# Joint attention: the samples' score products as sixteen tiles of 32 by 32 at once, over four PSUM banks

## The chip, the core and the metric

The kernel runs on one core of one Trainium2 chip. The metric is the device time of one execution, in microseconds. The kernel before took 3689.43 us in the median of three runs (3681.23 to 3694.0).

## The reference

One inference step of a two-layer streaming encoder. Layer 0 holds sliding-window attention beside differential attention (4 heads of two score maps each), layer 1 holds forgetting attention (16 heads), and each layer has a SwiGLU block. A prompt of 1024 new frames and 8 running sample streams go through the same weights. Each sample stream brings 16 new frames and a cache of 2048 keys and values. What the change touches is the sample side of the two global attentions:

```python
def _diff_attend(q, k, v, qpos, kpos, lam):          # layer 0, part B
    scores = jnp.einsum('bthed,bshed->bhets', q2, k2).astype(jnp.float32) * SCALE
    p = jax.nn.softmax(jnp.where(mask, scores, NEG_INF), axis=-1)
    attn = p[:, :, 0] - lam * p[:, :, 1]
    return jnp.einsum('bhts,bshd->bthd', attn.astype(v.dtype), v)

def _fox_attend(q, k, v, cq, ck, qpos, kpos):        # layer 1
    scores = jnp.einsum('bthd,bshd->bhts', q, k).astype(jnp.float32) * SCALE
    scores = scores + jnp.moveaxis(cq, 1, 2)[..., :, None] - jnp.moveaxis(ck, 1, 2)[..., None, :]
    p = jax.nn.softmax(jnp.where(mask, scores, NEG_INF), axis=-1)
    return jnp.einsum('bhts,bshd->bthd', p.astype(v.dtype), v)
```

The products meant by the title are `q k^T` of one stream's 16 frames, for eight half-heads or heads (128 rows), with its 2048 cached keys. In layer 1 a fifth product adds the forget bias.

## The kernel before

`joint_attention` is called twice: as `jb` (differential, `diff` true) and as `jc` (forgetting attention). It interleaves the prompt's attention of one head with the cached attention of one sample stream. Such a pair is called a unit `u` here: `U` is 8 in `jb` and 16 in `jc`. Each unit has S = 8 steps `s`, one for each 128-row tile of the prompt's head, in the order 3, 4, 2, 5, 1, 6, 0, 7. With n = 8u + s, a step issues on TensorE (PE): `score(n + 3)`, `turn(n + 1)` (transposes of the probabilities, groups of four into a slot of the ring `turned`, which has 2 PSUM banks), on odd steps `attend((n - 1) // 2)` (probabilities times values, for two tiles at once), on even steps `turn_back((n - 2) // 2)`.

The sample's work is put between these. In unit u the products with the cached keys (`score_keys`) run at s = 6 and 7, and the rest for that stream follows in unit u + 1: ScalarE (ACT) copies the scores to SBUF (`copy_scores`: the first pair at s = 7, the second at s = 0), VectorE (DVE) takes the maximum at s = 1, ACT the exponential at s = 2 and 3, PE transposes and multiplies by the values from s = 3 to s = 5 (`turn_probs`, `attend_sample`), DVE scales the output at s = 6 (`scale_output`), PE turns it at s = 7 (`turn_output`) and DVE copies it out at s = 7 (`copy_out`).

`score_keys(u, pair)` issues, for each of 4 (`jb`) or 5 (`jc`) inner steps, matmuls of 32 rows by 32 columns for the four column groups c and the two row groups a of the pair: eight tiles, into the two banks of `s_ps`. Each matmul of the code is two in the trace. The same two banks hold the sample's transposed probabilities and its output later, so the second pair waits for the copies of the first.

DVE also transposes the cached keys of the next stream by 32 by 32 blocks (`turn_keys`, 16 instructions for a unit): four at each of s = 5, 6 and 7, two at each of s = 3 and 4; unit 0 has six at s = 6 and at s = 7, and in the last unit there are none. Half of a step's transposes stand before `invert`, half after it, all in front of the next step's work:

```python
                    if n % 2 == 1:
                        output((n - 3) // 2)
                    if 1 <= u <= U and s == 6:
                        scale_output(u - 1)
                    maximum(n + 3)
                    turns = turns_at(u, s)
```

Each engine works in the order of its code. `attend(k)` waits for `out_done` 2k (L1517), that is for DVE's `output(k - 1)`, which stands at the head of DVE's same odd step and itself needs PE's `turn_back(k - 1)` of the step before. SyncE issues the loads of keys when `s_done` says that `score_keys` of two units back has ended, and the loads of values when `s_pv_done` says that `attend_sample` has.

## Time and profile before

| | us |
|---|---|
| runs: median (lowest to highest of 3) | 3689.43 (3681.23 to 3694.0) |
| span of the profiled execution | 3685.0 |
| PE busy (all) | 3411.1 (93%) |
| DVE busy | 1597.5 (43%) |
| ACT busy | 1123.5 (30%) |
| matmuls of L1556 (`score_keys`), busy, `jb` and `jc` | 59.6 and 123.3, with the bias's 38.0 |
| `jc`, from the first to the last block of `score_keys` | 537.95 |

The page is read from the top: PE is busy nearly the whole span, so the questions are which of PE's work becomes shorter, and what PE would wait for then. A group's busy time is the union of its instructions' spans, which overlap where tiles run side by side; so the length of a block is read from the starts in the timeline, not from the mean of one.

### The profile page before, as it was taken

The numbers are of one execution on the slowest core, as the hardware profiler recorded it, in microseconds if no ns is written. First come the engines' busy times: TensorE is split into PE (matmuls) and PEld (weight loads), VectorE is DVE, ScalarE is ACT, GpSimd is POOL, SyncE is SP. The second block draws the span as 40 slices with busy tenths as digits, with TensorE's granted clock in tenths as the row PEclk, the third lists the DMA queues.
The fourth block names the chain that finished last, engine by engine and source line by source line (L and its number), as shares of the span: only waits on it lengthen the run. The fifth ranks groups of instructions, "written<-read, shape, count | busy, mean of one in ns | idle before, by whom it ended". The sixth has DMA issues, their size and how long they took to land. (4 is left out here: it accounts for less than half of the span.)

```text
span 3685.0 us, 63062 instructions
## 1 busy us (share of the span) xinstructions
PE 3411.1 (93%) x25000; PEld 2914.6 (79%) x25000; DVE 1597.5 (43%) x2910; ACT 1123.5 (30%) x2343; POOL 254.4 (7%) x340
## 2 busy tenths in 40 slices
PE   8998599788999999997899799999988999999997
PEld 7876466577999999996789666666567999999996
DVE  5417477463333333336231266666533333333334
ACT  4215255443112112113222245555433211211211
POOL 2310000032000000004000000000013000000003
PEclk9999799999999999998999899999989999999999
DMA  5438599443111111112554599999644111111102
GB/s 170 127 122 181 168 336 309 159 161 119 36 34 57 34 46 34 39 41 92 154 174 124 148 317 320 303 308 329 213 149 137 43 37 34 57 34 46 34 29 102
DMA packets 399665, 493.23 MB, mean 134 GB/s; under 512 B 69744, under 2 KB 251536, under 8 KB 399312
## 3 DMA queue, kind: packets, MB, share of 16 engines
q1 hardware_dynamic: 399456, 490.36, 42.8%
q8 instruction: 141, 2.31, 0.3%
q14 instruction: 68, 0.56, 0.1%
HBM read 407.10 MB, written 84.10 MB: 133 GB/s over the span
## 5 line engine op out<-in xcount | busy, mean ns | idle before, releaser
L2546 DVE TENSOR_TENSOR f_gated<-f_gated,f_up 128x384 f32<-128x384 f32 x132 | 73.1, 554 | 734.8 <-ACT f_gated L2476 734.8
L2570 DVE TENSOR_TENSOR f_y<-f_y,f_down 128x512 f32<-128x512 f32 x396 | 269.5, 686 | 229.6 <-PE f_down L2665 229.5
L2652 PE MATMUL f_gate<-m_ht_hi,f_w_hi 128*128 128x384 f32 x1056 | 355.0, 336 | 12.1 <-DVE f_w_lo L2597 12.1
L2652 PE MATMUL f_gate<-m_ht_lo,f_w_hi 128*128 128x384 f32 x1056 | 354.5, 336 | 0.0
L2652 PE MATMUL f_gate<-m_ht_hi,f_w_lo 128*128 128x384 f32 x1056 | 354.5, 336 | 0.0
L2652 PE MATMUL f_up<-m_ht_hi,f_w_lo 128*128 128x384 f32 x1056 | 352.7, 334 | 0.0
L2652 PE MATMUL f_up<-m_ht_hi,f_w_hi 128*128 128x384 f32 x1056 | 352.7, 334 | 0.0
L2652 PE MATMUL f_up<-m_ht_lo,f_w_hi 128*128 128x384 f32 x1056 | 352.7, 334 | 0.0
L2665 PE MATMUL f_down<-f_wo_hi,f_act_hi 128*128 128x512 f32 x792 | 312.6, 395 | 10.7 <-DVE f_y L2570 9.3
L2665 PE MATMUL f_down<-f_wo_lo,f_act_hi 128*128 128x512 f32 x792 | 309.2, 390 | 0.0
L2665 PE MATMUL f_down<-f_wo_hi,f_act_lo 128*128 128x512 f32 x792 | 309.1, 390 | 0.0
L2476 ACT ACTIVATE f_gated<-f_gate 128x384 f32<-128x384 f32 x132 | 65.0, 493 | 684.6 <-PE f_up L2652 684.3
L2652 PEld LDWEIGHTS f_gate<-m_ht_hi,f_w_hi 128*128 128x128 f32 x1056 | 199.6, 189 | 13.7 <-issue 12.9
L2652 PEld LDWEIGHTS f_gate<-m_ht_lo,f_w_hi 128*128 128x128 f32 x1056 | 199.6, 189 | 0.8
L2652 PEld LDWEIGHTS f_gate<-m_ht_hi,f_w_lo 128*128 128x128 f32 x1056 | 199.5, 189 | 0.0
L2652 PEld LDWEIGHTS f_up<-m_ht_hi,f_w_lo 128*128 128x128 f32 x1056 | 198.2, 188 | 0.0
L2652 PEld LDWEIGHTS f_up<-m_ht_hi,f_w_hi 128*128 128x128 f32 x1056 | 198.2, 188 | 0.0
L2652 PEld LDWEIGHTS f_up<-m_ht_lo,f_w_hi 128*128 128x128 f32 x1056 | 198.2, 188 | 0.0
L2665 PEld LDWEIGHTS f_down<-f_wo_hi,f_act_hi 128*128 128x128 f32 x792 | 149.2, 188 | 52.6 <-DVE f_y L2570 19.0
L1822 DVE STREAM_TRANSPOSE jc_kc<-jc_kc 128x512 f32<-128x512 f32 x256 | 180.9, 706 | 16.8 <-DMA jc_kc<-in_cache_c_k 2.7
L2665 PEld LDWEIGHTS f_down<-f_wo_hi,f_act_lo 128*128 128x128 f32 x792 | 148.9, 188 | 31.6
L2665 PEld LDWEIGHTS f_down<-f_wo_lo,f_act_hi 128*128 128x128 f32 x792 | 149.0, 188 | 29.6
(394 smaller groups left out, 6698.8 us busy)
## 6 DMA issues: line engine op xcount, KB each, us to landing
jc_kc<-in_cache_c_k SPq DMA_DIRECT2D x64, 1024.0 KB, 10.5
jc_vc<-in_cache_c_v SPq DMA_DIRECT2D x64, 1024.0 KB, 10.3
jb_kc<-in_cache_b_k SPq DMA_DIRECT2D x32, 1024.0 KB, 11.6
jb_vc<-in_cache_b_v SPq DMA_DIRECT2D x32, 1024.0 KB, 11.1
m_raw<-in_w_ffn_in SPq DMA_DIRECT2D x44, 512.0 KB
f_raw<-in_w_ffn_in SPq DMA_DIRECT2D x44, 512.0 KB
f_raw_o<-in_w_ffn_out SPq DMA_DIRECT2D x22, 1024.0 KB, 6.4
m_raw<-x SPq DMA_DIRECT2D x18, 512.0 KB, 4.1
```

The source lines that it names most:

```text
L1822: dve.transpose(kc[:, u % 2, t, :], kc[:, u % 2, t + 1, :]).then_inc(kt_done, 1)
L2476: act.activation(silu[:, b], gate[:, q, 0:gw], ACT.Silu).then_inc(silu_done, 1)
L2546: dve.tensor_tensor(prod[:, b], silu[:, b], up[:, q, 0:gw], ALU.mult).then_inc(prod_done, 1)
L2570: dve.tensor_tensor(part, part, down[:, half, :], ALU.add).then_inc(added, 1)
L2652: last = pe.matmul(acc[:, q, 0:gw], a[:, s, k, u, :], b[:, k, token], start=(k == 0 and j == 0), stop=(k == KT - 1 and j == 2))
L2665: last = pe.matmul(down[:, half, :], a[:, s, t * P:(t + 1) * P], b[:, s, half * 512:(half + 1) * 512], start=(n == 0), stop=(n == 5))
```

## The change

`score_keys(u)` is called once, at s = 7, with all four row groups: sixteen tiles for each inner step, into four banks. Two of these are the banks of `s_ps`, two are slots of the ring `turned`, used under new keys `("sk", u, 0)` and `("sk", u, 1)`. ACT copies all four banks at s = 0 of the next unit, the ring's two first, ahead of that step's `copy_prompt`. `turn_output` goes from s = 7 to s = 6 and writes to `s_ps` instead of a ring slot, with semaphores of its own (`ot_done`, `ot_copied`). DVE's `copy_out` stays at s = 7 but goes ahead of that step's transposes, and `score_keys(u)` waits for it.

```diff
--- before.py
+++ after.py
@@ -1226,8 +1226,9 @@
             use_prompt(S * u + s + 1)
             if u < U and s == 5:
                 use(("sn", u), "act")
-            if 1 <= u <= U and s == 7:
-                use(("ot", u - 1), "dve", 1 if diff else 2)
+            if u < U and s == 7:
+                use(("sk", u, 0), "act")
+                use(("sk", u, 1), "act")
     use(("fin", 0), "dve")
     use(("fin", 1), "act")
     key_at = {r: key for key, r in seq.items()}
@@ -1267,9 +1268,10 @@
...
+         scaled, ot_done, ot_copied, s_stored) = (st.sem(n) for n in (
...
+        out_ops = 1 if diff else 2
@@ -1537,15 +1539,16 @@
                         last = pe.matmul(o_back[:, e * DH:(e + 1) * DH], src[0:held], halves[0:held], start=True, stop=True)
                 last.then_inc(back_done, 1)
 
-            def score_keys(u, pair):
-                if pair == 0:
-                    pe.wait_ge(kt_done, parts * per * (u + 1))
-                    if u:
-                        pe.wait_ge(scaled, u)
-                pe.wait_ge(s_copied, 4 * u + 2 * pair)
-                for step in range(4 if diff else 5):
+            def score_keys(u):
+                pe.wait_ge(kt_done, parts * per * (u + 1))
+                if u:
+                    pe.wait_ge(scaled, u)
+                    pe.wait_ge(ot_copied, out_ops * u)
+                banks = [ring_slot(("sk", u, 0)), ring_slot(("sk", u, 1)), s_ps[:, 0], s_ps[:, 1]]
+                n_steps = 4 if diff else 5
+                for step in range(n_steps):
                     for c in range(4):
-                        for a in (2 * pair, 2 * pair + 1):
+                        for a in range(4):
                             rows_a, hb = slice(Q * a, Q * a + Q), 4 * c + step
                             if step < 4:
                                 weights = q_blocks[rows_a, hb // 2, hb % 2]
@@ -1553,10 +1556,11 @@
                             else:
                                 weights = select[rows_a, Q * c:Q * c + Q]
                                 moving = bias[rows_a, u % 2, 0:bank].rearrange("p (t r) -> p t r", r=Q)
-                            last = pe.matmul(s_ps[Q * c:Q * c + Q, a % 2].rearrange("p (t r) -> p t r", r=Q), weights, moving,
-                                             start=(step == 0), stop=(step == (3 if diff else 4)), skip_group_check=True,
+                            last = pe.matmul(banks[a][Q * c:Q * c + Q].rearrange("p (t r) -> p t r", r=Q), weights, moving,
+                                             start=(step == 0), stop=(step == n_steps - 1), skip_group_check=True,
                                              tile_position=(Q * a, Q * c))
-                last.then_inc(s_done, 1)
+                            if step == n_steps - 1 and c == 3:
+                                last.then_inc(turn_done if a < 2 else s_done, 1)
 
             def score_new(u):
                 if u == 0:
@@ -1584,7 +1588,7 @@
             def turn_probs(u, gi):
                 a, b = PG[gi]
                 pe.wait_ge(s_exp_done, 2 * u + (1 if b <= per * 2 else 2))
-                pe.wait_ge(s_copied, 4 * (u + 1))
+                pe.wait_ge(s_copied, 2 * (u + 1))
                 if gi >= 2:
                     pe.wait_ge(pt_copied, len(PG) * u + (1, 3, 4)[gi - 2])
                 for t in range(a, b):
@@ -1596,7 +1600,7 @@
             def attend_sample(u, part):
                 pe.wait_ge(pt_copied, len(PG) * u + (2, 4)[part])
                 if part == 0:
-                    pe.wait_ge(s_copied, 4 * (u + 1))
+                    pe.wait_ge(s_copied, 2 * (u + 1))
                 else:
                     pe.wait_ge(vnew_loaded, 16 * (u + 1))
                 for t in ((range(0, 2 * per), range(2 * per, tiles))[part]):
@@ -1615,7 +1619,8 @@
 
             def turn_output(u):
                 pe.wait_ge(scaled, u + 1)
-                pe.transpose(ring_slot(("ot", u))[:, 0:P], o_rows[:], ident[:]).then_inc(turn_done, 1)
+                pe.wait_ge(pt_copied, len(PG) * (u + 1))
+                pe.transpose(s_ps[:, 0, 0:P], o_rows[:], ident[:]).then_inc(ot_done, 1)
 
             pe.wait_ge(setup, 10)
             score(0)
@@ -1637,18 +1642,18 @@
                     if 1 <= u <= U and s == 5:
                         turn_probs(u - 1, 4)
                         attend_sample(u - 1, 1)
-                    if u < U and s >= 6:
-                        score_keys(u, s - 6)
+                    if u < U and s == 7:
+                        score_keys(u)
                     if n % 2 == 0:
                         turn_back((n - 2) // 2)
                     if 1 <= u <= U and s == 4:
                         attend_sample(u - 1, 0)
                         turn_probs(u - 1, 2)
-                    if 1 <= u <= U and s == 7:
+                    if 1 <= u <= U and s == 6:
                         turn_output(u - 1)
             for part in range(2):
                 slot = ring_slot(("fin", part))
-                wait_emptied([("ot", U - 1)])
+                pe.wait_ge(ot_copied, out_ops * U)
                 for j in range(pairs // 2):
                     last = pe.transpose(slot[:, j * P:(j + 1) * P], out_t[:, part * pairs // 2 + j, :], ident[:])
                 last.then_inc(turn_done, 1)
@@ -1702,13 +1707,17 @@
                     act.wait_ge(back_done, k)
                 act.activation(o_turn[:], pv[:, 0:2 * P], ACT.Copy).then_inc(o_copied, 1)
 
-            def copy_scores(u, pair):
-                act.wait_ge(s_done, 2 * u + pair + 1)
+            def copy_scores(u, a):
+                if a < 2:
+                    act.wait_ge(turn_done, seq[("sk", u, a)] + 1)
+                else:
+                    act.wait_ge(s_done, 2 * (u + 1))
                 if u:
                     act.wait_ge(pt_done, len(PG) * u)
-                for a in (2 * pair, 2 * pair + 1):
-                    act.activation(s_scores[:, 0:PAST].rearrange("p (t a r) -> p a t r", a=4, r=Q)[:, a],
-                                   s_ps[:, a % 2].rearrange("p (t r) -> p t r", r=Q), ACT.Copy).then_inc(s_copied, 1)
+                dst = s_scores[:, 0:PAST].rearrange("p (t a r) -> p a t r", a=4, r=Q)[:, a]
+                src = turned[:, seq[("sk", u, a)] % ring] if a < 2 else s_ps[:, a - 2]
+                act.activation(dst, src.rearrange("p (t r) -> p t r", r=Q), ACT.Copy).then_inc(
+                    act_emptied if a < 2 else s_copied, 1)
 
             def copy_new_scores(u):
                 if u:
@@ -1733,18 +1742,20 @@
             for u in range(U + 1):
                 for s in range(S):
                     n = S * u + s
-                    if u < U and s == 7:
-                        copy_scores(u, 0)
                     exponential(n + 2)
                     if n % 2 == 0:
                         copy_output((n - 2) // 2)
                     if u >= 1 and s == 3:
                         exponential_sample(u - 1, 1)
+                    if u >= 1 and s == 0:
+                        copy_scores(u - 1, 0)
+                        copy_scores(u - 1, 1)
                     copy_prompt(act, n + 1)
                     if diff and u == 0 and s == 7:
                         exponential_lambda()
                     if u >= 1 and s == 0:
-                        copy_scores(u - 1, 1)
+                        copy_scores(u - 1, 2)
+                        copy_scores(u - 1, 3)
                     if u >= 1 and s == 2:
                         exponential_sample(u - 1, 0)
                     if u >= 1:
@@ -1828,11 +1839,13 @@
                 dve.transpose(ktn, kn).then_inc(ktn_done, 1)
 
             def maximum_sample(u, x):
-                dve.wait_ge(s_copied, 4 * u + 2 * x + 2)
+                if x == 0:
+                    dve.wait_ge(act_emptied, count[("sk", u, 1)])
+                else:
+                    dve.wait_ge(s_copied, 2 * (u + 1))
                 if u and x == 0:
                     dve.wait_ge(s_exp_done, 2 * u)
                 if x == 0:
-                    dve.wait_ge(act_emptied, count[("sn", u)])
                     dve.tensor_reduce(s_neg[:, 2:3], s_scores[:, PAST:], AX.X, ALU.max, negate=True).then_inc(s_max_done, 1)
                 part = s_scores[:, 0:PAST].rearrange("p (t x n) -> p x t n", x=2, n=2 * Q)[:, x]
                 dve.tensor_reduce(s_neg[:, x:x + 1], part, AX.XY, ALU.max, negate=True).then_inc(s_max_done, 1)
@@ -1850,7 +1863,7 @@
                 dve.wait_ge(s_pv_done, u + 1)
                 dve.wait_ge(s_inv_done, u + 1)
                 if u:
-                    dve.wait_ge(turn_done, seq[("ot", u - 1)] + 1)
+                    dve.wait_ge(ot_done, u)
                 if diff:
                     dve.tensor_scalar(o_rows[:], o_ps, s_inv[:, u % 2:u % 2 + 1], weight[:], ALU.mult,
                                       ALU.mult).then_inc(scaled, 1)
@@ -1858,19 +1871,19 @@
                     dve.tensor_scalar(o_rows[:], o_ps, s_inv[:, u % 2:u % 2 + 1], None, ALU.mult).then_inc(scaled, 1)
 
             def copy_out(u):
-                key, g = ("ot", u), u // STREAMS
-                o_turn = turned[:, seq[key] % ring, 0:P].rearrange("p (j e f) -> p j e f", j=4, e=2)
-                dve.wait_ge(turn_done, seq[key] + 1)
+                g = u // STREAMS
+                o_turn = s_ps[:, 0, 0:P].rearrange("p (j e f) -> p j e f", j=4, e=2)
+                dve.wait_ge(ot_done, u + 1)
                 if diff:
                     dve.tensor_copy(o_first_head[:], o_turn[:, :, 0, :]).then_inc(o_half, 1)
                     dve.wait_ge(o_half, u + 1)
                     dve.tensor_tensor(out_t[:, 4 * g:4 * g + 4, frames_of(u)], o_first_head[:], o_turn[:, :, 1, :],
-                                      ALU.add).then_inc(dve_emptied, 1)
+                                      ALU.add).then_inc(ot_copied, 1)
                 else:
                     for hd in range(2):
                         part = slice(DH * hd, DH * hd + DH)
                         dve.tensor_scalar(out_t[part, 4 * g:4 * g + 4, frames_of(u)], o_turn[part, :, hd, :], 1.0, None,
-                                          ALU.mult).then_inc(dve_emptied, 1)
+                                          ALU.mult).then_inc(ot_copied, 1)
 
             def products_lambda():
                 dve.wait_ge(lam_loaded, 32)
@@ -1898,6 +1911,8 @@
                     if 1 <= u <= U and s == 6:
                         scale_output(u - 1)
                     maximum(n + 3)
+                    if 1 <= u <= U and s == 7:
+                        copy_out(u - 1)
                     turns = turns_at(u, s)
                     for v, t in turns[:len(turns) // 2]:
                         turn_keys(v, t)
@@ -1919,8 +1934,6 @@
                     invert(n)
                     for v, t in turns[len(turns) // 2:]:
                         turn_keys(v, t)
-                    if 1 <= u <= U and s == 7:
-                        copy_out(u - 1)
             copy_turned(dve, ("fin", 0), s_out[:, 0:pairs * P // 2], turned[:, seq[("fin", 0)] % ring, 0:pairs * P // 2])
 
 
```

## Rows read from the trace of the kernel before

**Rows 1.** the page: granted TensorE clock in 40 slices, in tenths

```profile
PEclk9999799999999999998999899999989999999999
```

**Rows 2.** windows: length, busy of PE, PEld, DVE, ACT, POOL; clock, DMA share, GB/s

```profile
2128.25:2666.20 537.95, 518.43 (x7536) 340.12 (x7543) 346.98 (x781) 281.95 (x693) 0.00 (x0) 0.99 0.94 299
```

**Rows 3.** timeline of PE, jc, steps 6, 7: start, duration, ..., [idle before]

```profile
2311.66 3.66 PE L1556 MATMUL jc_s_ps<-jc_kc,jc_q_blocks 32*32 32x512 f32 x64
2315.12 1.06 PE L1556 MATMUL jc_s_ps<-jc_bias,jc_select 32*32 32x512 f32 x16
2316.11 0.66 PE L1537 MATMUL jc_pv<-jc_halves,jc_o_turn 128*128 128x64 f32 x4
...
2317.63 1.30 PE L1522 MATMUL jc_pv<-jc_probs_t,jc_vp 128*64 128x256 f32 x16
2318.86 3.66 PE L1556 MATMUL jc_s_ps<-jc_kc,jc_q_blocks 32*32 32x512 f32 x64
...
2323.31 0.33 PE L1618 MATMUL jc_turned<-jc_ident,jc_o_rows 128*128 128x128 f32 x1
```

**Rows 4.** timeline of PEld (weight loads), jc, start of a block

```profile
2128.25 0.18 PEld L1556 LDWEIGHTS jc_s_ps<-jc_kc,jc_q_blocks 32*32 32x32 f32 x16 [0.17 <-issue]
```

**Rows 5.** timeline of DVE, jc, the same steps 6 and 7

```profile
2310.88 0.82 DVE L1768 TENSOR_REDUCE jc_neg_top<-jc_scores_b 128x1 f32<-128x640 f32 x1 [0.54 <-PE jc_scores_b L1496]
...
2313.25 1.53 DVE L1822 STREAM_TRANSPOSE jc_kc<-jc_kc 128x512 f32<-128x512 f32 x2
2316.81 0.48 DVE L1803 TENSOR_SCALAR jc_out<-jc_pv,jc_inv 128x64 f32<-128x64 f32 x2 [2.03 <-PE jc_pv L1537]
...
2323.68 0.48 DVE L1872 TENSOR_SCALAR jc_out_t<-jc_turned 64x64 f32<-64x64 f32 x2 [2.76 <-PE jc_turned L1618]
```

**Rows 6.** timeline of PE, jb: a block at step 6 and what follows

```profile
562.79 3.66 PE L1556 MATMUL jb_s_ps<-jb_kc,jb_q_blocks 32*32 32x512 f32 x64
566.38 0.44 PE L1534 MATMUL jb_pv<-jb_ident,jb_o_turn 128*128 128x128 f32 x2
...
567.61 2.23 PE L1522 MATMUL jb_pv<-jb_probs_t,jb_vp 128*128 128x256 f32 x16
```

**Rows 7.** timeline of PE, jb, step 7 of unit 0

```profile
462.20 2.23 PE L1522 MATMUL jb_pv<-jb_probs_t,jb_vp 128*128 128x256 f32 x16 [0.62 <-DVE jb_out L1803]
```

**Rows 8.** timeline of DVE, jb, beside rows 6

```profile
564.49 1.52 DVE L1822 STREAM_TRANSPOSE jb_kc<-jb_kc 128x512 f32<-128x512 f32 x2
566.86 0.61 DVE L1799 SCALAR_TENSOR_TENSOR jb_out<-jb_pv,jb_inv_lam,jb_out 128x128 f32<-128x128 f32 x2 [0.85 <-PE jb_pv L1534]
```

**Rows 9.** timeline of ACT, jc: the copies of both pairs of scores

```profile
2316.29 1.09 ACT L1710 ACTIVATE jc_s_scores<-jc_s_ps 128x512 f32<-128x512 f32 x2 [3.81 <-PE jc_s_ps L1556]
...
2325.61 1.09 ACT L1710 ACTIVATE jc_s_scores<-jc_s_ps 128x512 f32<-128x512 f32 x2
```

**Rows 10.** timeline of PE, jc, step 3: first transposes of probabilities

```profile
2331.38 1.09 PE L1593 MATMUL jc_s_ps<-jc_ident,jc_s_scores 128*128 128x128 f32 x8 [0.90 <-ACT jc_s_scores L1723]
```

**Rows 11.** windows: five single units, columns as in rows 2

```profile
2139.90:2174.04 34.14, 33.24 (x499) 22.13 (x491) 22.73 (x50) 18.68 (x46) 0.00 (x0) 1.00 1.05 320
2289.11:2323.31 34.20, 33.30 (x500) 22.28 (x493) 23.20 (x52) 18.68 (x46) 0.00 (x0) 1.00 0.93 302
2323.31:2357.65 34.34, 33.44 (x501) 22.30 (x494) 23.20 (x52) 18.68 (x46) 0.00 (x0) 1.00 1.01 323
573.40:607.60 34.20, 32.94 (x449) 23.98 (x444) 23.70 (x52) 18.74 (x46) 0.00 (x0) 1.00 1.04 341
607.60:642.10 34.50, 33.07 (x451) 24.03 (x444) 25.16 (x60) 18.79 (x46) 0.00 (x0) 1.00 0.93 300
```

**Rows 12.** timeline of PE, jc: two idle stretches before a matmul

```profile
2226.63 0.21 PE L1578 MATMUL jc_turned<-jc_turned_new,jc_q_blocks 32*32 32x16 f32 x3 [2.13 <-issue]
...
2236.05 6.21 PE L1556 MATMUL jc_s_ps<-jc_kc,jc_q_blocks 32*32 32x512 f32 x54 [1.86 <-issue]
```

**Rows 13.** window after the second of these, columns as in rows 2

```profile
2236.00:2249.00 13.00, 12.95 (x98) 5.38 (x100) 2.78 (x8) 3.02 (x7) 0.00 (x0) 0.50 1.00 257
```

3 lines of the change are left out of this document (1 added, 2 removed).

## The prediction

> **What bounds the kernel now.** The windows over the `jc` stage come first [rows 2]: PE is busy 518 of 538 us, the DMA engines have a share of 0.94, DVE 347 us, ACT 282 us. So PE sets the time, and DMA is the next. The timeline of PE over steps 6 and 7 of one unit is the second view [rows 3]. The reader is to see two blocks of `score_keys`, each 4.45 us from its own start to that of the next work (2311.66 to 2316.11, 2318.86 to 2323.31). Five inner steps of two matmuls each give ten rounds of eight tiles, and the rows of 64 and 16 matmuls are ten times eight. In `jb` there are eight rounds and a block takes 3.59 us (562.79 to 566.38) [rows 6]. The difference of two rounds is 0.86 us, so a round costs 0.43 us, and 0.15 us or so of a block is its start. The granted clock is 1.00, its upper level of 2.4 GHz, in every single unit read [rows 11]; the slices of the whole span show it a little lower only here and there [rows 1].
>
> **What the change removes.** The sixteen tiles of an inner step run in one round where they were two of eight. If the array takes the four row groups at once as it now takes two, one of the two blocks of a unit is gone whole: 4.45 us in each of 16 units of `jc`, 3.59 us in each of 8 of `jb`, 71.2 + 28.7 = 99.9 us of PE time. No row shows four row groups at work. What speaks for it: four banks are written by four row groups, one each, as two are by two now, and sixteen weight loads of this shape go in 0.18 us [rows 4], less than half of a round. I take one round for sixteen, 0.43 us; the other end is 0.86 us, as before.
>
> The Trainium skill ("TensorEngine Tiling (Array Packing)", sections "Tiling Modes" and "Restrictions and Gotchas") says that the 32 by 32 mode has sixteen tiles which load and multiply in parallel, and that different row tiles must write to different PSUM banks, which the change obeys. By it the block is halved as above; no run here shows it yet. The same page ("PSUM Bottleneck") warns that the copies out of PSUM may then become the bound.
>
> **Where it is put, and what was hidden there.** The block that goes is, in time, the one at step 6, because all tiles now run at step 7. It covered DVE. At step 7 `attend` waits for DVE's `output`, which stands behind four key transposes of step 6. Before, the pair of transposes at 2313.25 ended at 2314.78, the block ended at 2316.11, and DVE was idle for 2.03 us until `turn_back` gave it work [rows 5]. Now PE passes from the end of step 6's `turn` (2311.66) to `attend` in the time that `turn_back`, `score` and `turn` took, 2317.63 - 2316.11 = 1.52 us, and 0.09 us for `turn_output`: it is there at 2313.27. DVE is free at 2314.78, `output` takes 0.48 us [rows 5], and about 0.1 us passes until PE starts: 2315.36. PE waits 2.1 us, so a unit of `jc` gains 4.45 - 2.1 = 2.35 us.
>
> In `jb` PE reaches `attend` at 562.79 + (567.61 - 566.38) + 0.09 = 564.11 [rows 6]. The transposes end at 566.01 and `output` takes 0.61 us [rows 8], so PE starts at about 566.7: 2.6 us of wait, and a gain of 3.59 - 2.6 = 1.0 us. That this wait is real shows in unit 0 of `jb`, where six transposes stand at step 6: PE already waits 0.62 us for `output` there, with the block still in place [rows 7].
>
> **The units at the ends.** Unit 0 has six transposes at that place, so in `jb` nothing is gained and in `jc` I take 0.5 us. The last unit has none, so the whole block is gained: 4.45 and 3.6 us. The sum: `jc` 14 x 2.35 + 4.45 + 0.5 = 37.9 us, `jb` 6 x 1.0 + 3.6 + 0 = 9.6 us, together 47.5 us.
>
> **What is moved, and its cover.** `copy_out` (0.48 us [rows 5]) now stands ahead of step 7's transposes, and the block waits for it. DVE does `output` until 2315.3, a maximum over 384 columns (0.82 us for 640, so about 0.5) and `copy_out` until 2316.3; PE's `attend` runs from 2315.36 for 1.23 us to 2316.6. So this costs nothing, with a margin of 0.3 us in `jc`; in `jb` `attend` is 0.9 us longer [rows 6] and the margin over 1 us. Were the margin gone, it would cost at most the 0.5 us a unit, 11 us in all. Step 7's transposes are later by 0.48 us and still end before step 0's maximum is due. `turn_output` at step 6 waits for `scaled`, which DVE gives before its maximum at 2310.88; nothing.
>
> ACT copied the first pair under the second block (idle before it 3.81 us), and the second 2.30 us after that block's end, behind `copy_prompt` [rows 3, 9]. Now all four copies follow the block. A pair takes 1.09 us. The ring's two start 0.18 us after the end, as at 2316.29 after 2316.11, and are done at 1.27 us. PE meanwhile has step 0's `score` to do, needs the first slot only then, and the second four transposes later, so it waits less than that 1.27 us, and I take nothing. `copy_prompt` then copies two groups; at the 0.55 us of one of these copies it is done by 2.37 us, and the other pair at 3.46 us behind the block, where it ended 3.39 us behind it before (2326.70 - 2323.31). So the chain over DVE's maximum to ACT's exponential, which lets PE wait 0.90 us at step 3 [rows 10], keeps its length. Bounds: nothing, or the 1.09 us of the pair in each of 24 units, 26 us. I take nothing, because the later end comes out the same.
>
> The skill's warning on the copies would make those 26 us the result; the rows on ACT speak against it, since ACT is busy 18.7 of 34.2 us of a unit [rows 11].
>
> **DMA, the next bound.** A window under steady load shows a share of 1.05 [rows 11], so I take that as full. Two `jc` units in a row have 0.93 and 1.01, thus 31.7 us of full load for each on the mean; two of `jb` 1.04 and 0.93, thus 32.2 us. The forecast makes a unit 34.2 - 2.35 = 31.9 us in `jc` and 33.3 us in `jb`. It just fits. The loads have buffers for a unit ahead, so I take nothing here, but DMA is the reason why a larger gain would not come through: if the wait for `output` were not there, units would stop at 31.7 and 32.2 us, a gain of 2.6 and 2.1 us each.
>
> **Clock.** PE now idles for 2.1 to 2.6 us in 20 units. In this trace the clock held at 1.00 over 2.13 us of idle; the next idle, listed with 1.86 us, was followed by 0.50, its lower level of 1.2 GHz, for 13 us [rows 12, 13]. Half of that, 6.5 us, is lost by one such fall. So the new idle stretches lie just where the trace shows both results. Bounds: no fall, or one in each of the 20 units, 130 us. I take one in five, 4 falls, as the first row held and the second had that idle 10 us ahead of it; and 4 us for each, since the new block has half as many rounds to slow. That is 16 us, an estimate.
>
> **The sum.** 47.5 - 16 = 31.5 us. From the profiled 3685.0 us that gives a span of 3653.5 us; the median of the runs lies 4.4 us above that span, so the forecast is 3689.4 - 31.5 = 3658 us.
>
> **The rivals.**
> A. Less of the wait, DMA at the limit. If PE waits less for DVE than I think, DMA stops the gain: 15 x 2.6 + 4.45 + 7 x 2.1 + 3.6 = 61.8 us, and no fall of the clock: 3628 us. For it speaks that the wait is worked out and seen only in unit 0; against it the fixed order of DVE's work.
> B. The clock falls often. Place: the wait at step 7. Price 6.5 us for each fall; from 7 falls on nothing is left of the gain, and with 14 the time is 3689.4 - 47.5 + 91 = 3733 us, slower than before. For it speaks [rows 12, 13]; against it that 2.13 us held.
> C. Sixteen tiles take two rounds, so the change doesn't do what it says. The block then takes the time of two, nothing is removed but the start of one (0.15 us a unit), and the wait for `output` remains new: 14 x 2.1 + 6 x 2.6 - 24 x 0.15 = 41 us more, 3731 us. It turns slower from a round of about 0.63 us on (47.5 us over 24 units is 2.0 us, over 8 to 10 rounds 0.2 us).
> D. The pieces cancel: 4 to 7 falls at full price, or the copies on the chain (26 us), leave 3680 to 3695 us.
>
> **How the numbers follow.** Forecast 0.60, A 0.15, B 0.08, C 0.07, D 0.10. The range goes from A's time to where D ends, 3628 to 3695 us, which leaves out B and C. The bound for faster and slower is 0.3%, about what a measurement of this kernel can tell from no change: 3678 and 3700 us. Faster: forecast and A, 0.75. Slower: B and most of C, 0.14. Same: 0.11.
>
> **What would show it right or wrong.** One block of `score_keys` a unit, with 128 and 32 matmuls merged, 4.45 us long in `jc` and 3.6 in `jb` (C: 8.7 us). At step 7 `attend` with an idle of about 2.1 us (2.6 in `jb`) before it, released by DVE's `output`, in all units but the last (A: under 1 us). The wait at step 3 still 0.9 us. A `jc` unit of 31.9 us with a DMA share near 1.05 (A: waits for DMA appear on DVE's transposes). The granted clock under 1.00 in some windows of single units (B: in most). The prediction is wrong at its root if `attend` at step 7 does not wait, or if the block is not halved.

## The result: 3697 us, a little slower than before

The changed kernel takes 3697.0 us (median of 18 runs, 3691.5 to 3707.5) where the kernel before takes 3688.8 us (18 runs, 3679.8 to 3698.7): a ratio of 1.0026, 95% interval 1.0017 to 1.0036. The forecast was 3658 us with a range to 3695, so it missed, on the side of slower. The profiled execution has a span of 3696.7 us (3685.0 before), and the page's slices of the granted clock stand against [rows 1]:

```profile
core 0: 3696.7 us, clock 0.955
PEclk9999699989999999998899889999989999999999
```

Two windows answer to [rows 2]: from the end of the first block of `score_keys` to the end of the last one, in `jb` (7 units) and in `jc` (15 units). Columns as in rows 2. The kernel before (from the end of its first pair of blocks):

```profile
467.95:709.81 241.86, 230.28 (x3087) 166.42 (x3079) 161.97 (x382) 128.99 (x315) 0.00 (x0) 1.00 0.88 290
2139.90:2667.27 527.37, 507.85 (x7373) 335.32 (x7365) 337.45 (x763) 277.95 (x683) 0.00 (x0) 0.99 0.94 299
```

The changed kernel:

```profile
472.76:717.13 244.37, 215.01 (x3084) 169.05 (x3080) 161.01 (x384) 129.69 (x315) 0.00 (x0) 0.99 0.85 281
2151.77:2679.56 527.79, 471.56 (x7370) 338.24 (x7365) 334.65 (x765) 282.16 (x683) 0.00 (x0) 0.96 0.92 295
```

The halving is there: PE is busy 36.3 us less in `jc` and 15.3 us less in `jb`. But the stretches are as long as before (+0.4 and +2.5 us), because PE's idle time went from 19.5 to 56.2 us and from 11.6 to 29.4 us. The waits of PE in the `jc` window say for whom (total us, times, longest). Before:

```profile
PE jc_s_ps L1593 <- ACT jc_s_scores L1723: 13.5, 15, 0.9
PE jc_s_ps L1556 <- issue: 2.2, 2, 1.9
PE jc_turned L1578 <- issue: 2.1, 1, 2.1
PE jc_s_ps L1611 <- issue: 0.9, 2, 0.6
PE jc_pv L1522 <- DVE jc_out L1803: 0.7, 1, 0.7
```

After, the four largest:

```profile
PE jc_pv L1524 <- DVE jc_out L1814: 28.6, 15, 2.2
PE jc_s_ps L1597 <- ACT jc_s_scores L1732: 13.5, 15, 0.9
PE jc_turned L1559 <- issue: 5.2, 4, 2.4
PE jc_s_ps L1559 <- issue: 4.0, 3, 2.3
```

The wait for ACT is the same 13.5 us. The wait of `attend` for DVE's `output` is new, 27.9 us more. "issue", the wait for nothing that the profile shows, goes from 5.2 to 13.9 us over all its rows. One unit of `jc` shows both (timeline of PE, steps 6 and 7, as in [rows 3]):

```profile
2358.87 0.61 PE L1507 MATMUL jc_turned<-jc_ident,jc_probs 128*128 128x128 f32 x4
2361.64 1.11 PE L1524 MATMUL jc_pv<-jc_probs_t,jc_vp 128*64 128x256 f32 x14 [2.17 <-DVE jc_out L1814]
...
2369.01 0.62 PE L1559 MATMUL jc_turned<-jc_kc,jc_q_blocks 32*32 32x512 f32 x2 [1.77 <-issue]
...
2371.09 0.50 PE L1496 MATMUL jc_scores_b<-jc_k_both,jc_q_hi 128*128 128x512 f32 x1
```

DVE beside it, as in [rows 5]:

```profile
2357.99 1.52 DVE L1833 STREAM_TRANSPOSE jc_kc<-jc_kc 128x512 f32<-128x512 f32 x2
2359.43 0.12 DVE L1788 RECIPROCAL jc_inv<-jc_total 128x1 f32<-128x1 f32 x1
2359.61 1.53 DVE L1833 STREAM_TRANSPOSE jc_kc<-jc_kc 128x512 f32<-128x512 f32 x2
2361.07 0.43 DVE L1814 TENSOR_SCALAR jc_out<-jc_pv,jc_inv 128x64 f32<-128x64 f32 x2
```

`output` stands behind four key transposes, and `attend` starts 0.57 us after `output` does: the predicted wait, 2.17 us where 2.1 was forecast. The block then has a stop of 1.77 us in its middle, for nothing that the profile names; and this block of sixteen tiles takes 8.24 us in all, where a block of eight took 4.45. The stop costs more than its idle time: an undisturbed block is 5.45 us (below), 1.77 more make 7.22, and this one is another 1.02 us longer at a granted clock of 1.00. Over the stops in blocks at full clock, in this kernel and in e1_turns, that surplus is 0.5 to 1.0 us each.

**A round of sixteen.** An undisturbed block, the last of `jc`, shows what is left when nothing stops it (timeline of PE; the first tile of each of the first four rounds, and the work behind the block):

```profile
2674.12 0.62 PE L1559 MATMUL jc_turned<-jc_kc,jc_q_blocks 32*32 32x512 f32 x2
...
2674.57 0.59 PE L1559 MATMUL jc_turned<-jc_kc,jc_q_blocks 32*32 32x512 f32 x2
...
2675.00 0.80 PE L1559 MATMUL jc_turned<-jc_kc,jc_q_blocks 32*32 32x512 f32 x2
...
2675.43 0.80 PE L1559 MATMUL jc_turned<-jc_kc,jc_q_blocks 32*32 32x512 f32 x2
...
2679.57 0.69 PE L1539 MATMUL jc_pv<-jc_halves,jc_o_turn 64*128 64x64 f32 x3
```

It takes 2679.57 - 2674.12 = 5.45 us, 1.00 us more than the 4.45 of a block of eight; in `jb` it is 4.39 for 3.59 us. All sixteen do run at once. But ten rounds need 5.45 and eight need 4.39, so a round is 0.53 us on the mean, not 0.43. The first tiles of the rounds shown still follow each other by 0.43 to 0.45 us; from the third round on it is the tiles behind them that come late. The weight loads show where (timeline of PEld, same block):

```profile
2674.57 0.10 PEld L1559 LDWEIGHTS jc_turned<-jc_kc,jc_q_blocks 32*32 32x32 f32 x1 [0.23 <-issue]
2675.00 0.29 PEld L1559 LDWEIGHTS jc_turned<-jc_kc,jc_q_blocks 32*32 32x32 f32 x2 [0.33 <-issue]
2675.21 0.10 PEld L1559 LDWEIGHTS jc_s_ps<-jc_kc,jc_q_blocks 32*32 32x32 f32 x1
```

Before, in a block of eight tiles:

```profile
2311.66 0.18 PEld L1556 LDWEIGHTS jc_s_ps<-jc_kc,jc_q_blocks 32*32 32x32 f32 x16 [0.17 <-issue]
2312.11 0.12 PEld L1556 LDWEIGHTS jc_s_ps<-jc_kc,jc_q_blocks 32*32 32x32 f32 x3 [0.28 <-issue]
2312.41 0.28 PEld L1556 LDWEIGHTS jc_s_ps<-jc_kc,jc_q_blocks 32*32 32x32 f32 x13 [0.18 <-issue]
```

With eight tiles a whole group of sixteen loads (0.18 to 0.28 us) is done under the matmuls ahead of it. With sixteen, one single load goes ahead (2674.57) and one more at 2675.00; the others begin only some 0.2 us later, when the matmuls before have ended, and then loads and matmuls come one pair after another.

The Trainium skill ("TensorE: Matmul & The Clock Gate", section "Part 3: Packing small matmuls — row/col tiling") says that PE pulls weight loads ahead of running matmuls out of a window of 64 instructions. Two rounds of sixteen are 32 loads and 32 matmuls, 64 instructions, and two rounds of eight are 32; the rows agree with that, without showing the window itself. A rival, that the array or the banks are slower with more than eight tiles and the loads only follow, is not excluded by these rows.

### The profile page after: what moved, and what is told of

Read it like the earlier page. It is cut to its first block and busy times, and to the rows that moved or that the text cites. A ratio compares the mean times of both kernels' runs of the same rounds, so it can differ in the third digit from the quotient of the medians.

```text
span 3696.7 us, 63126 instructions
## 1 busy us (share of the span) xinstructions
PE 3363.5 (91%) x25000; PEld 2928.5 (79%) x25000; DVE 1591.8 (43%) x2910; ACT 1128.8 (31%) x2343; POOL 254.8 (7%) x340
## 3 DMA queue, kind: packets, MB, share of 16 engines
q8 instruction: 141, 2.31, 0.3%
## 5 line engine op out<-in xcount | busy, mean ns | idle before, releaser
L2665 PEld LDWEIGHTS f_gate<-m_ht_hi,f_w_hi 128*128 128x128 f32 x1056 | 199.6, 189 | 13.7 <-issue 12.9
L2678 PEld LDWEIGHTS f_down<-f_wo_hi,f_act_lo 128*128 128x128 f32 x792 | 149.2, 188 | 31.5
```

Source lines behind the costliest of these rows:

```text
L2665: last = pe.matmul(acc[:, q, 0:gw], a[:, s, k, u, :], b[:, k, token], start=(k == 0 and j == 0), stop=(k == KT - 1 and j == 2))
L2678: last = pe.matmul(down[:, half, :], a[:, s, t * P:(t + 1) * P], b[:, s, half * 512:(half + 1) * 512], start=(n == 0), stop=(n == 5))
```

## The experiments

Times are medians, ratios are against the kernel before on the same chip. "Stage" is the `jc` window from the end of the first block to that of the last, 15 units: 527.4 us before, 527.8 us after. Three theories on where the 39 us between forecast and result went are tested: W, sixteen tiles at once leave no room for weight loads ahead, so a round is 0.53 us; C, the wait for `output` also makes the clock fall; F, the stops inside the blocks are waits for instructions, whose fetches the bulk loads delay.

**e1_turns: the four transposes moved away.** The table of key transposes alone is changed, so that none stands ahead of `output` at step 6:

```
-    ahead = {5: range(0, 4), 6: range(4, 8), 7: range(8, 12), 3: range(12, 14), 4: range(14, 16)}
+    ahead = {5: range(0, 4), 7: range(4, 12), 3: range(12, 14), 4: range(14, 16)}
```

> The four key transposes that DVE did at step 6 are done at step 7, behind copy_out and under the block of score products. Theory D (DVE's output stands behind these transposes, PE waits for it ahead of attend, and the wait makes the clock fall): the wait of 2.18 us in jc and 2.5 to 2.6 us in jb goes to under 0.5 us in all units but the first, where six transposes stay at step 6. The falls of the clock inside the two stages (2 in jb, 12 in jc, 3.4 us each) go to 3 or fewer. About 38 us of waits and 14 x 1.7 = 24 us of clock come back: 3697 - 60 = 3637 us, between 3625 and 3655. Rival (DMA is the bound of both kernels in these stages, so the units stay at 34 to 35 us whatever PE waits for): the same wait appears elsewhere, on DVE for keys or on PE for values, and the time stays within 3690 to 3700 us.

Measured 3662.2 us (3658.6 to 3670.8, 4 runs), ratio 0.993 (0.9911 to 0.9949): faster than both kernels. The wait of `attend` is gone in every unit but the first and last of a stage. So the wait was caused by the order of DVE's work. But 25 us of the expected gain are missing: the stage takes 509.2 us.

```profile
2132.91:2642.12 509.21, 463.65 (x7371) 335.33 (x7366) 339.56 (x765) 280.95 (x683) 0.00 (x0) 0.98 0.96 305
```

The stops inside the blocks have grown. The longest (timeline of PE):

```profile
2161.26 0.60 PE L1559 MATMUL jc_turned<-jc_kc,jc_q_blocks 32*32 32x512 f32 x2
2165.68 0.62 PE L1559 MATMUL jc_s_ps<-jc_kc,jc_q_blocks 32*32 32x512 f32 x2 [3.82 <-issue]
```

"issue" now sums to 31.2 us in the stage. During this stop, 2161.9 to 2165.6, the DMA queues show (packets, MB, share):

```profile
q1 hardware_dynamic: 388, 0.81, 100.5%
q8 instruction: 1, 0.02, 2.3%
```

One fetch of the instruction queue falls into it (its 1.35 us lie between 2163.0 and 2164.4, as narrower windows show), between bulk packets that fill the DMA engines. The places of the stops are regular: behind matmul 84, 91, 98, 105, 113, 120, 127, 134, 142, 149 and 156 of the block's 160 in units 1 to 11; the changed kernel, where it stops, does so at the same ones. A unit has 492 loads, 492 matmuls and 25 or 26 semaphore instructions, about 1010; 14 or 15 are missing to 1024, and the stop moves by seven matmuls and their loads in each unit. So the stops stand where PE has used up a multiple of 256 instructions; not every multiple has one. Counted through this stage, all 19 idle stretches marked "issue" of more than 0.3 us stand at the same remainder of 256, within one instruction, and PE goes on 1.3 to 1.6 us after a fetch has landed. This is theory F: **PE stops for want of instructions.**

The kernel before has such stops too. Its five of more than 0.3 us in this stage stand at the same remainder, and the two of [rows 12] are among them; about the first of these (idle from 2224.50; window 2223.9 to 2226.6) the queues show:

```profile
q1 hardware_dynamic: 511, 1.02, 102.1%
q8 instruction: 1, 0.02, 2.4%
```

The prediction read [rows 12] for the clock alone, and did not ask why PE stood there.

The Trainium skill ("Runtime: NRT & Kernel Launch", section "Instruction fetch mechanics") says that instructions are refilled in blocks of 16 KiB, 256 instructions, and that crossing a boundary is mostly hidden. The first agrees with the page's 141 fetches of 2.31 MB and the places of the stops; the second does not hold in the dense blocks here, where up to 3.8 us are not hidden.

**e5_light: less DMA traffic.** The changed kernel with the loads of cached keys and values cut to one tile of four from the third unit on.

```
-                    sp.dma_start(kc[:, u % 2, 1 + per * x:1 + per * (x + 1)],
+                    more = per if u < 2 else 1
+                    sp.dma_start(kc[:, u % 2, 1 + per * x:1 + per * x + more],
...
```

> From unit 2 on each load of cached keys and values brings one 128-row tile of four, a quarter of the bytes, so most rows of the caches are stale ones. All instructions of PE, ACT and DVE are the same. Theory F1 (the fetch of PE's instructions waits behind the bulk loads on the DMA engines): the stops of 1.3 to 2.4 us inside the jc blocks go away in units 2 to 15, the blocks are 5.45 us as in the last unit, where nothing is loaded, and jc becomes shorter by 14 x 1.5 = 21 us. Theory F2 (the stops come from the pace of 320 instructions in 5.5 us alone, whatever the DMA engines do): they stay, and the blocks are 6.5 to 7.4 us. Theory W: the rounds of sixteen tiles stay at 0.53 us in both cases. The wait for DVE's output stays at 2.18 us and the clock still falls.

Measured 3670.9 us (one run). The stage:

```profile
2145.31:2652.31 507.00, 459.84 (x7370) 338.85 (x7366) 334.71 (x765) 282.14 (x683) 0.00 (x0) 0.97 0.50 137
```

"issue" falls from 13.9 to 2.5 us, while the wait for DVE stays (31.0 us). The stops hang on the load of the DMA engines: the expectation's F1 holds, F2 falls. The clock still falls, 9 times, so the stops are not what makes it fall.

**e10_before_light: the same cut in the kernel before.**

```
-                    sp.dma_start(vc[:, x], v_cache[stream_of(u), x * span:(x + 1) * span, columns_of(u)].rearrange(
+                    more = per if u < 2 else 1
+                    sp.dma_start(vc[:, x, 0:more], v_cache[stream_of(u), x * span:x * span + more * P, columns_of(u)].rearrange(
...
```

> The kernel before with the loads of cached keys and values cut to one tile of four from the third unit on; left out: three quarters of the cached rows' loads. Beside e5_light (the changed kernel so, 3671 us) and e7_turns_light (3617 us) it gives what each is worth where the DMA engines are half idle. Theory L (the full DMA engines held before back a little as well, and took most of what the change saved): before with light loads 3675 to 3685 us, a cached unit of 34.1 us, so that the change alone is worth some 10 us and with the transposes moved some 60 us. Rival (before was held by the DMA engines too, as much as the others): 3650 us or less.

Measured 3682.8 us (one run), as the theory had it; the rival falls. The stage:

```profile
2142.39:2663.86 521.47, 504.25 (x7372) 334.63 (x7364) 337.34 (x763) 278.04 (x683) 0.00 (x0) 0.99 0.49 135
```

With the DMA engines half idle, the kernel before gains 6 us and the changed one 26. The change is then worth 11.9 us instead of costing 8. These are single runs, and the runs of one kernel lie up to 19 us apart, so the sizes are rough (the 6 us is within that spread); but the stages say the same, 521.5 us here against 507.0 in e5_light.

**e7_turns_light: e1_turns with the light loads.** Both edits together.

> The kernel e1_turns with the loads of cached keys and values cut to one tile of four from the third unit on, so that most cached rows are stale ones of an earlier unit. Left out: three quarters of the cached rows' loads. It gives what TensorE's side alone takes. Theory (stops come with the full DMA engines, waits of the attend with the four transposes, the fall of the clock with that wait): no stops, no waits, blocks 4.39 and 5.45 us nearly throughout, at most 2 falls of the clock in the last 16 units, a unit of them about 31 us, 3635 us in all (3625 to 3650). Rival (the clock falls for another reason than the waits): the same 9 falls as with the light loads alone, and 3655 us or more.

Measured 3617.4 us (one run), 18 us below what was expected. The stage:

```profile
2125.59:2598.95 473.36, 450.86 (x7370) 332.75 (x7366) 339.41 (x765) 280.52 (x683) 0.00 (x0) 0.99 0.53 147
```

"issue" is 8.1 us, the clock falls once, and a unit takes 31.6 us. With light loads, moving the transposes is worth 53.5 us; with full loads 34.8.

**e11_turns_threequarters: three tiles of four.** As e7_turns_light, with `more` = 3.

> The kernel e1_turns with three tiles of four loaded of the cached keys and values; left out: a quarter of the cached rows' loads. DMA bytes of a unit go from 10.6 to 8.6 MB, so that by 316 GB/s a unit needs 27 us of the DMA engines where it needed 33.5. Theory L (a bound by the bytes): as fast as with one tile of four, the stage of the last 16 units 480 to 487 us, 3617 to 3625 us in all. Rival (contention that grows with the traffic, without a bound): in the middle between 3617 and 3662, some 3635 to 3650 us.

Measured 3637.0 us (one run). The stage:

```profile
2129.39:2620.82 491.43, 456.81 (x7370) 332.64 (x7365) 339.54 (x765) 280.88 (x683) 0.00 (x0) 0.99 0.83 260
```

It is in the middle: at a DMA share of 0.83 "issue" is still 20.5 us. In the stages of e1_turns, e5_light, e7_turns_light and this run neither PE nor DVE waits for a load. So a bound by bytes is not what holds e1_turns: theory L falls here, its rival holds. PE's feed suffers with the traffic, at a share of 0.53, 0.83, 0.96 with 8, 20 and 31 us.

What of a fetch becomes slower can be read by setting the fetches beside the count of instructions. Those of one fetch take nearly as long in every case (median 1.06 us in e7_turns_light, 1.11 in e11 and e1_turns). What grows is the time from PE's passing one multiple of 256 to the start of the next fetch: median 1.8, 3.0 and 3.7 us, and 8.9 us ahead of the stop of 3.82 us in e1_turns. Whether the fetch is asked for late or stands in a queue behind the bulk loads, the trace doesn't show.

**e6_aligned: no-operations to move the boundary.** e1_turns with `pe.nop()` added, 68 once and 14 in each unit.

> The kernel e1_turns (the four transposes that wait for VectorE's output go to the next step), with no-operation instructions on TensorE in the cached stage of the last 16 units: 68 at its start and 14 in each unit, so that a unit has 1024 instructions of TensorE, four times the 256 that one fetch of the instruction queue brings, and the boundary between two fetches stays at the same place, some 50 matmuls into the block. Theory F (the stops of 1.3 to 4.4 us in the blocks are waits for the next fetch, and they come only where the boundary falls into the second half of a block): nearly all blocks of these units take 5.45 us and the time is about 3635 us (3625 to 3650), unless the DMA engines, at a share of 0.99 already, become the bound. Rival (the stops have another cause, such as the data of the caches): the blocks keep 7 to 10 us and the time stays at 3662 us or a few us above it for the 220 added instructions.

Measured 3663.6 us (3661.2 to 3669.4, 4 runs), ratio 0.9933 (0.9913 to 0.9952). The trace has none of the no-operations: the counts of a unit are unchanged and the stops stand at the same matmuls, 84, 91, 98. It tells nothing of F and is a repetition of e1_turns.

**e9_fill_aligned: the same with real instructions.**

```
+                if not diff and u < U - 1:
+                    for _ in range(41 if u == 0 else 7):
+                        pe.transpose(s_ps[:, 0, 0:Q], o_rows[0:Q], ident[0:Q, 0:Q])
                 pe.transpose(s_ps[:, 0, 0:P], o_rows[:], ident[:]).then_inc(ot_done, 1)
```

> The kernel e1_turns with real instructions where e6_aligned's no-operations had vanished: small transposes (32 rows, 32 columns) that nothing needs, in the cached stage of the last 16 units, 41 of them ahead of the turned output of the first unit and 7 in each unit after it, so that a unit has 1024 instructions of TensorE and the boundary between two fetches stays some 50 matmuls into each block. Theory F (the place of the boundary makes the stops): the stops inside the blocks of these units go, blocks 5.45 us, and the stage gets shorter than the 516 us of e1_turns by about 20 us or more. Theory L (the DMA engines, at a share of 0.98, are the bound, and the stops only take up time that would be waited for elsewhere): the stops go, but the stage stays at 516 us within 6, since as much is then waited for at other places. Rival to both: the stops stay where they were in number of matmuls.

Measured 3663.6 us (3660.4 to 3669.9, 4 runs), ratio 0.9923 (0.9906 to 0.9941). The stops left the blocks: 12 of 15 take 5.45 or 5.46 us, the others 7.29, 5.48 and 5.66. Yet the stage takes 512.4 us. The waits of PE:

```profile
PE jc_pv L1539 <- issue: 18.0, 10, 3.0
PE jc_s_ps L1597 <- ACT jc_s_scores L1735: 13.5, 15, 0.9
PE jc_pv L1524 <- DVE jc_out L1817: 4.4, 3, 2.9
PE jc_s_ps L1625 <- DVE jc_o_rows L1874: 1.5, 1, 1.5
PE jc_s_ps L1615 <- DMA jc_vc<-in_cache_c_v: 1.0, 1, 1.0
```

The stops stand now at L1539, `turn_back` right behind the block, ten times up to 3.0 us: 256 instructions after a boundary some 50 matmuls into the block is a place just behind it. So theory F is shown to be right on the mechanism, since adding 14 instructions a unit moved and fixed the stops where the count says. It was wrong on the price: "issue" goes from 31.2 only to 19.3 us, and the 139 added transposes (11.4 us busy), 6.4 us of waits for DVE and DMA that e1_turns had not (its 0.5 us left out) and more falls of the clock (8 for 4) take that back. Added up, these are more than the 3.2 us by which the stage is longer than that of e1_turns, so they are no exact account.

The waits of DVE show something new in this stage, which e1_turns had not at all:

```profile
DVE jc_kc L1836 <- DMA jc_kc<-in_cache_c_k: 19.3, 9, 3.5
DVE jc_out L1817 <- DMA o_c<-jc_out: 11.4, 4, 6.0
```

DVE waits for the loads of keys and for stores of `jc_out`. From the first to the last block it is 518.4 us, where e1_turns has 516.1: the figure that theory L gave (516 within 6). So at full traffic (share 0.97) the data come late as soon as PE's stops have left the blocks, and one limit takes the place of the other. How much of it the 139 added transposes make, this run doesn't tell.

**e8_fill: work in place of the wait.** The changed kernel with 17 unneeded transposes at step 6.

```
+                for _ in range(17):
+                    pe.transpose(s_ps[:, 0, 0:P], o_rows[:], ident[:])
                 pe.transpose(s_ps[:, 0, 0:P], o_rows[:], ident[:]).then_inc(ot_done, 1)
```

> The changed kernel with 17 repeated transposes of the probabilities put ahead of the attend's wait for VectorE's output, about 2 us of TensorE's work that nothing needs. Theory C (each wait of 2.2 us lets the clock fall to half, and a fall costs about 1.7 us more): the waits go from 2.18 to about 0.2 us, the falls of the clock inside the cached stage from 14 to at most 3, and the time goes down by some 20 us against the changed kernel, to about 3676 us (3668 to 3685). Rival (the falls cost nothing on the path, or come from elsewhere): 3697 us within 5, or more where the added work doesn't fit into the wait.

Measured 3689.8 us (3682.0 to 3693.4, 10 runs), ratio 1.0001 (0.9991 to 1.0010), so some 9 us less than the changed kernel's 1.0026. The stage:

```profile
2146.84:2673.65 526.81, 490.39 (x7625) 366.40 (x7621) 335.43 (x765) 282.51 (x683) 0.00 (x0) 0.98 0.93 296
```

The wait goes from 28.6 to 4.4 us, the recorded stretches at half clock from 12 with 41.0 us to 4 with 23.9 us. So the waits did make the clock fall in most units. But the stage is only 1 us shorter: the falls saved 8.6 us, "issue" took 4.6 us back (13.9 to 18.5), and the filling work was about 3 us longer than the waits it filled. The expected 20 us did not come. By the spans, 7.4 of the 8.2 us between the two profiled executions lie outside both stages, where next to nothing was changed; so single profiles don't show what makes up the 9 us.

**e2_eight: same places and banks, eight tiles at once.** At step 7 the two pairs run one after the other.

> The same four banks and the same places as the changed kernel, but row groups 0 and 1 run all inner steps first and then 2 and 3: eight tiles at once instead of sixteen. Theory W (weights are not loaded ahead any more when one inner step has 16 tiles, 64 instructions): the rounds are 0.43 us each, the block is 2 x 8 x 0.43 + 0.15 = 7.0 us in jb and 8.7 us in jc. Theory F (in jc the instructions of the dense block arrive late): no stop inside the block, as it takes 320 instructions in 8.7 us and not in 5.5, so the jc blocks are 8.7 us with at most one or two exceptions. Against the changed kernel jb loses 8 x 2.3 = 18 us and jc 16 x 1.4 = 22 us: 3735 us, 3715 to 3750. Rival A (more than eight tiles at once run no faster than eight): the blocks are no longer than in the changed kernel, 4.4 and 7 us, and the time stays at 3697 us.

Measured 3801.1 us (3781.8 to 3819.6), ratio 1.0309 (1.0258 to 1.0361), slower than expected. An undisturbed block takes 8.18 us in `jc` and 6.46 in `jb`, so sixteen at once save 2.7 and 2.1 us of it. The surprise is the clock. A stretch of 10.2 us with the block in it (windows):

```profile
2245.41:2255.65 10.24, 10.24 (x114) 3.41 (x118) 2.86 (x5) 1.20 (x5) 0.00 (x0) 0.50 0.73 267
```

In the changed kernel a fall ends within its block:

```profile
2469.16:2472.57 3.41, 3.41 (x57) 1.54 (x70) 2.82 (x5) 0.60 (x3) 0.00 (x0) 0.50 1.04 389
2472.57:2475.72 3.15, 3.15 (x106) 1.96 (x78) 0.00 (x0) 0.00 (x0) 0.00 (x0) 1.00 1.04 382
```

Once fallen behind the wait, the clock mostly stays at its lower level of 1.2 GHz through a block of eight-tile rounds (10 stretches, 119.5 us in the stage, eight of them 10.2 to 27.3, two 3.4) and comes back in 3.4 us in the changed kernel (12 stretches, 41.0 us). That the number of tiles makes the difference is not shown: e3_rows_outer below has sixteen, and still four stretches of 10.2 to 13.7 us, which begin inside its blocks and run on behind them. And with eight tiles "issue" is 5.3 us in the stage, as little as before, at a DMA share of 0.81.

**e4_twelve: column group 3 only in the first inner step.** Left out: most products of a quarter of the score rows, so that the rounds have twelve tiles.

> The last column group takes part in the first inner step only, so that inner steps 2 to 5 have twelve tiles instead of sixteen. This leaves out most of the products of a quarter of the score rows. Theory W: a step of twelve tiles is 48 instructions, so 16 of the 64 that PE has before it belong to the step after, and the weights of about four tiles are loaded ahead, in the time of the running round, where one was with sixteen tiles and all eight with eight. The rounds of the later steps lie between 0.43 us and the 0.53 us of sixteen tiles. Rival A (the array or the PSUM banks are slower with more than eight tiles): the weights of the twelve tiles are loaded at the same intervals as those of sixteen, with one ahead, and a round is longer by the number of tiles over eight: 0.48 us.

Measured 3676.8 us (one run). Undisturbed blocks take 5.05 us in `jc` and 4.20 in `jb`, 0.60 us over the eight-tile blocks where sixteen are 1.00 and 0.80 over. The excess shrinks with the number of tiles, and the last rounds of twelve come 0.43 us apart; but the first inner step still has sixteen, so this doesn't single out a number of tiles. It doesn't decide between the theories either: with 0.53 us for the first two rounds the other eight are 0.48 us on the mean, the figure of rival A. For W speak the weight loads. From 1.72 to 2.07 us after the start of the last block seven begin here and three in the changed kernel.

**e3_rows_outer: the other order of issue.**

```
-                        for c in range(4):
-                            for a in range(4):
+                        for a in range(4):
+                            for c in range(4):
```

> The changed kernel with the sixteen tiles of an inner step issued row group by row group, four column groups inside, where it has column group by column group. Theory W (a round of sixteen takes 0.53 us because its 64 instructions fill what TensorE can hold, so that the next weights are not loaded ahead): the same blocks, 4.39 and 5.45 us where nothing stops them, and again one load ahead of its round. Rival (the order of issue makes tiles of one row group or of one bank get in each other's way): the undisturbed blocks change by more than 0.2 us, to 3.6 and 4.45 at best. Time by theory W 3697 us within 8.

Measured 3713.0 us (one run), 8 us above what theory W allowed. The last block (timeline of PE):

```profile
2689.89 0.66 PE L1559 MATMUL jc_turned<-jc_kc,jc_q_blocks 32*32 32x512 f32 x8
...
2695.34 0.80 PE L1539 MATMUL jc_pv<-jc_halves,jc_o_turn 64*128 64x64 f32 x4
```

It takes 5.45 us again, and 4.39 in `jb`: the order doesn't matter for a round, so a conflict of row groups or banks through it falls. The longer time has other causes: 12 stretches at half clock with 71.7 us instead of 41.0, and "issue" at 17.3 us instead of 13.9. Why the stretches last longer stays open.

**e12_unit0: the first units too.** e1_turns with all twelve transposes of the first unit's steps 6 and 7 at step 7.

```
-            return [(1, t) for t in range(6 * s - 36, 6 * s - 30)]
+            return [(1, t) for t in (range(0, 12) if s == 7 else ())]
```

> The kernel e1_turns, and in the first unit of each stage the twelve key transposes of steps 6 and 7 all at step 7, so that attend's wait there (4.37 and 3.37 us) goes too. Theory (the waits are made by where the transposes stand): both waits under 0.5 us, and 4 to 8 us less than e1_turns, about 3656 us (3652 to 3661), the fastest so far. Rival (the transposes are then late for unit 1, or hold back the maximum of step 0 behind them): PE waits elsewhere in unit 0 or 1 and the time stays at 3662 us or more.

Measured 3662.8 us (3657.0 to 3665.4, 5 runs), ratio 0.9933 (0.9919 to 0.9947). The waits of 4.37 and 3.37 us are gone as expected, the time isn't: the same as e1_turns. In its `jc` stage PE now waits 2.5 us in two places for `output`, and the block of unit 1 takes 12.5 us for 11.8. In `jb` the stage is 7.2 us longer than in e1_turns (236.3 for 229.1), with a wait of 2.97 us for `output` at its start and 9.1 us of "issue" for 5.6.

## Why the prediction was wrong, step by step

**Right: the wait.** `attend` waits for `output`: 2.17 or 2.18 us in 12 of the 14 middle units of `jc` (2.1 forecast), 2.5 to 2.85 in `jb` (2.6). Over the two stages, without their first units, the wait for DVE grew by 27.9 and 15.6 us, 43.5 in all, where the sum held 14 x 2.1 + 6 x 2.6 = 45.0. e1_turns shows its cause.

**Right: the copies and the ring.** The wait at step 3 is still 0.9 us, 13.5 us in the stage.

**Right in size, wrong in form: the clock.** The sum held 4 falls of 4 us, 16 us. There were 14 recorded stretches with 47.8 us at half, thus 23.9 us lost, and 6.9 us (13.7 at half) of before are gone: 17.0 us net. Rival B had the number of falls (14) but at 6.5 us each; a fall now costs 1.7 us. That the term came out is luck: three and a half times the falls at less than half the price.

**Failed: "I take one round for sixteen, 0.43 us".** This is the term of the sum that was mis-sized most. A round takes 0.53 us. The weight loads of [rows 4] were seen with an idle engine ahead of them; whether they would still go ahead of running matmuls at twice the number was not asked. They do not: behind the second round most of them wait for the matmuls before. In the 15 and 7 units it costs 15 x 1.00 + 7 x 0.80 = 20.6 us.

**Failed: DMA, "It just fits".** It does, for the data, as long as PE's stops hold it back; e9 shows loads coming late once they have left the blocks. What it left out is that PE's instructions come over the same DMA engines. "issue" in the two stages went from 5.6 to 16.5 us, 10.9 us that no term held, with five such stops standing in the `jc` stage of before, two of them in [rows 12]. The same sentence bounded a kernel without the wait at 31.7 us a unit; e1_turns needs 33.9, and e7_turns_light, with light loads, 31.6.

**Failed: the first units.** The forecast was no gain in `jb` and 0.5 us in `jc`. The span up to the end of the first block of `jb` (of the first pair before) is 4.8 us longer, and from the end of `jb` to that of the first block of `jc` 4.5 us. `attend` waits 4.37 and 3.09 us there and the blocks take 4.93 and 7.19 us. The clock falls with these waits: in `jb` the `attend` after it takes 4.11 us where it took 2.16. From the start of step 6's `turn_back` (before: of the first block) to the end of the last block of the unit it is 3.4 and 2.8 us longer than before, though it holds one block less. The other 3 us lie in the work ahead of that, which changes by some 2 us from run to run.

**The account.** Forecast gain 31.5 us; less 20.6 (rounds), 10.9 (issue), 9.8 (first units with the 0.5) and 1.0 (clock), plus 1.5 (waits): -9.3 us. Measured on the spans: -11.7 us. So 2.4 us stay unassigned. The 0.5 to 1.0 us that a stop inside a block costs beside its idle time (nine such stops) would more than fill them, so some terms overlap and the account is good to a few us.

**The rivals.** A is a kernel without the wait; e1_turns is one, and gives 3662 us where A had 3628, for the rounds and the fetches cost it more than DMA's bound; e9 shows that bound right behind them. C falls: e2_eight shows what two rounds cost, 8.18 us a block against 5.45. D named the region next to the result, 3680 to 3695, for other reasons, and its sum was off: 4 to 7 falls at 6.5 us give 3668 to 3687 us, the copies on the chain 3684, and only 4 falls and the copies together 3694. So no single one of its causes reached the upper end of the range.

**What is shown and what is argued.** Shown: the wait and its cause (e1), the stops' link to DMA traffic (e5, e7, e11) and to the count of instructions (e9), the round of 0.53 us whatever the order (e3). Argued only: that the limit on loads ahead is the length of a window of instructions, and not an array that is slower with more than eight tiles; and that the fetch waits behind the bulk loads and is not asked for late. Open: how much of the full-traffic gain the data's own bound would take once the instructions come in time (e9). Had the four transposes moved with the block, the change would have given 27 us, 0.7%.

## What to carry to other kernels

When a block of PE work is taken out or put elsewhere, move with it the other engines' work that it covered: here one line, the place of four transposes, decided between 8 us lost and 27 us gained. Count instructions as well as time: work that issues more instructions per microsecond beside full DMA engines can wait for its own instructions. A row of before can warn of it: idle stretches marked "issue" of 1 to 2 us, as in [rows 12], that stand a multiple of 256 instructions apart and end about 1.5 us after a packet of the instruction queue. And a rate read at one number of tiles in flight (0.43 us for eight) is not the rate at twice the number; the weight loads between rounds are the row to look at.

## What was not expected of the hardware

- Sixteen tiles of 32 by 32 at once: 0.53 us a round against 0.43 for eight (1.00 us in a block of ten rounds); one weight load goes ahead of a round where a whole group does with eight.
- PE stops of up to 3.8 us at multiples of 256 instructions, ending 1.2 to 1.8 us after a fetch has landed, with "issue" of 8.1, 20.5 and 31.2 us in 15 units at DMA shares of 0.53, 0.83 and 0.96. Inside a block of products a stop cost 0.4 to 1.0 us more than its idle time.
- The clock, once at 1.2 GHz, stayed there for stretches of 10.2 to 27.3 us over most blocks of eight-tile rounds (e2_eight) and returned after 3.4 us in the changed kernel; but with sixteen tiles in another order (e3_rows_outer) four stretches lasted 10.2 to 13.7 us.
- `pe.nop()` left no instruction in the trace and moved no stop.
